# Latent attention interleaved one slice per product step, over four output and two gate chunks

## The reference, cut to what matters

```python
q, k = ...                    # 8 heads of 64 + 32 columns (the 32 rotated)
z = einsum("bhqd,bshd->bhqs", q_blk, k) * 96 ** -0.5
p = softmax(where(key_chunk <= q_chunk, z, -inf))
o_mla = einsum("bhqs,bshd->bhqd", p, v)
y_sb  = (o_sb  * silu(gate_sb))  @ w_o_sb
y_mla = (o_mla * silu(gate_mla)) @ w_o_mla
g = sigmoid(gate_logits + b_gate).reshape(b, s, 2, D_MODEL)
merged = g[:, :, 0] * y_sb + g[:, :, 1] * y_mla
x = x + merged @ w_out
```

## Time and profile before

| What | Value |
|---|---|
| median of three runs | 1740.01 us |
| the three runs | 1741.44, 1740.01, 1737.16 us |
| span of the profiled execution, first to last instruction | 1738.7 us |
| median less that span | 1.3 us |
| TensorE busy, share of the span | 96% |
| VectorE, ScalarE, GpSimd busy | 62%, 41%, 5% |
| mean granted TensorE clock | 0.981 |

### The profile page before, as it was taken

The page is one execution under the profiler, slowest core; times in us unless marked ns, Lnnn a source line. Parts: engine busy times, 40 slices in busy tenths (PEclk is TensorE's granted clock), DMA queues, the critical chain, the costliest instruction groups (busy, mean ns, idle before and its releaser), DMA issues.

```text
span 1738.7 us, 25519 instructions
## 1 busy us (share of the span) xinstructions
PE 1660.7 (96%) x9824; PEld 1332.2 (77%) x9824; DVE 1077.4 (62%) x1680; ACT 718.1 (41%) x1084; POOL 90.7 (5%) x130
## 2 busy tenths in 40 slices
PE   5979999999999999999989999999999999999997
PEld 2868787888888868777668888888887778876786
DVE  8899877665566765565655554455685563666443
ACT  4423434332333334444443332233546773655331
POOL 0063210000000000000000000000000000000000
PEclk9989999999999999999989999999999999999998
DMA  8342662434433444342222222322322211211231
GB/s 352 99 113 75 231 218 97 145 133 155 171 145 127 162 136 171 121 137 95 70 79 89 96 86 92 109 98 77 103 97 73 73 61 56 85 55 38 86 120 49
DMA packets 48821, 198.79 MB, mean 114 GB/s; under 512 B 8112, under 2 KB 13072, under 8 KB 35424
## 3 DMA queue, kind: packets, MB, share of 16 engines
q1 hardware_dynamic: 36064, 154.52, 25.8%
q0 software_dynamic: 12672, 43.10, 7.5%
HBM read 192.71 MB, written 4.23 MB: 113 GB/s over the span
## 4 chain that ended last, share of the span: by engine, by line
PE 82%; DVE 5%; ACT 5%; issue 5%; DMA 2%; POOL 1%; SPq 1%; DVEq 0%; ACTq 0%; POOLq 0%
PE ps L524 25%; PE ps L526 24%; PE ps L525 24%; ACT w_hi L983 2%; PE ps L630 2%; PE ps L643 2%; PE ps L655 2%; DMA ada<-in_ada_k 1%; PE ps L798 1%; ACT pw L1094 1%; POOL Mtz L341 1%; DVE w_lo L1454 1%; PE ps L591 1%; PE ps L774 0%; ACT sq L1085 0%
## 5 line engine op out<-in xcount | busy, mean ns | idle before, releaser
L524 PE MATMUL ps<-xn_hi,w_lo 128*128 128x512 f32 x1248 | 502.1, 402 | 11.0 <-DVE xn_lo L1604 9.2
L526 PE MATMUL ps<-xn_hi,w_hi 128*128 128x512 f32 x1248 | 491.1, 394 | 0.0
L525 PE MATMUL ps<-xn_lo,w_hi 128*128 128x512 f32 x1248 | 490.9, 393 | 0.0
L1454 DVE TENSOR_TENSOR w_lo<-raw,w_hi 128x2048 fp32r<-128x2048 f32 (+4 forms) x146 | 309.5, 2122 | 194.3 <-ACT w_hi L983 194.1
L983 ACT ACTIVATE w_hi<-raw 128x2048 fp32r<-128x2048 f32 (+4 forms) x147 | 260.9, 1775 | 175.2 <-PE ps L526 165.6
L524 PEld LDWEIGHTS ps<-xn_hi,w_lo 128*128 128x128 f32 x1248 | 237.5, 190 | 67.9 <-issue 18.5
L526 PEld LDWEIGHTS ps<-xn_hi,w_hi 128*128 128x128 f32 x1248 | 237.2, 190 | 50.8
L525 PEld LDWEIGHTS ps<-xn_lo,w_hi 128*128 128x128 f32 x1248 | 237.8, 191 | 46.2
L526 PE MATMUL ps<-act_hi,w_hi 128*128 128x512 f32 x352 | 136.9, 389 | 0.0
L524 PE MATMUL ps<-act_hi,w_lo 128*128 128x512 f32 x352 | 136.9, 389 | 0.0
L525 PE MATMUL ps<-act_lo,w_hi 128*128 128x512 f32 x352 | 136.9, 389 | 0.0
(11 more groups left out here) (396 smaller groups left out, 2430.9 us busy)
## 6 DMA issues: line engine op xcount, KB each, us to landing
raw<-in_weights SPq DMA_DIRECT2D x95, 1024.0 KB, 4.9
adaw<-in_ada_w POOLq DMA_DIRECT2D x64, 512.0 KB, 4.6
raw<-in_weights SPq DMA_DIRECT2D x18, 768.0 KB, 4.1
raw<-in_weights SPq DMA_DIRECT2D x16, 640.0 KB, 3.8
ada<-in_ada_k SPq DMA_DIRECT2D x8, 1024.0 KB, 17.9
rot<-in_ada_w POOLq DMA_DIRECT2D x16, 512.0 KB, 5.3
fbias<-f_dram SPq DMA_DIRECT2D x16, 256.0 KB, 4.0
raw<-in_weights SPq DMA_DIRECT2D x8, 512.0 KB, 3.6
```

Source lines behind the costliest of these rows:

```text
L524: pe.matmul(bank, lo_w, hi_x, start=start, stop=False)
L525: pe.matmul(bank, hi_w, lo_x, start=False, stop=False)
L526: return pe.matmul(bank, hi_w, hi_x, start=False, stop=stop)
L1454: V.tensor_tensor(w_lo[:, slot, w], raw[:, slot, w], f32(w_hi[:, slot, w]), ALU.subtract).then_inc(split_lo, 1)
```

## The change

On TensorE every product step is now followed by exactly one slice, over `osb_0` to `osb_3`, `g1_0` and `g1_1`: step, A, step, B, step, C. After the first slice that is issued ahead, 53 slices go with the first 53 of 64 steps. `g1_1` moves ahead of `omla_0`; `omla_1` follows `omla_0`; then `g1_2`, `omla_2`, `g1_3`, `omla_3` as before.

The splits move: `osb_1`, `osb_2`, `osb_3` to periods 1, 3, 6; `g1_0` to period 8 on ACT and in halves to periods 8 and 9 on DVE; `g1_1` to period 12, whole, on both; `omla_0` behind period 16 on ACT and behind period 17 on DVE. `branch_out` of the output chunks follows periods 4, 6, 9 and 12. The sigmoid of odd gate chunks goes to `nt` instead of `hn`. Behind the attention, ACT and DVE split `omla_1` ahead of the merging of 0, and `g1_2` behind it.

```diff
-for _m in range(4):
+LAYERS += [("g1_0", 8, 256, 1), ("g1_1", 8, 256, 1), ("omla_0", 4, 256, 1), ("omla_1", 4, 256, 1)]
+for _m in (2, 3):
     LAYERS += [(f"g1_{_m}", 8, 256, 1), (f"omla_{_m}", 4, 256, 1)]
...
+SPLIT_AT = (1, 3, 6, 8, 12)
...
+    def second_gate(m):
+        return (hn, nt)[m % 2]
...
         next(beats)
-        steps = [0]
         def between():
-            for _ in range(1 + steps[0] % 2):
-                next(beats, None)
-            steps[0] += 1
+            next(beats, None)
...
-        for m in range(4):
-            layer(f"g1_{m}", xn_hi, xn_lo, between=None if m else between)
-            if m == 0:
-                for _ in beats:
-                    pass
-            layer_part(f"omla_{m}", 0, mla_out(0), mla_out(1), (gm_lo, GATED["gate_mla"]) if m == 0 else None)
+        for m in range(2):
+            layer(f"g1_{m}", xn_hi, xn_lo, between=between)
+        for m in range(2):
+            layer(f"omla_{m}", mla_out(0), mla_out(1), (gm_lo, GATED["gate_mla"]) if m == 0 else None)
+        for m in range(2, 4):
+            layer(f"g1_{m}", xn_hi, xn_lo)
+            layer(f"omla_{m}", mla_out(0), mla_out(1))
...
         for n in range(18):
-            following = FIRST["osb_0"] + n // 4
-            mla_period(n, later=(lambda: split_next(following)) if n in (2, 6, 10, 14, 17) else None)
-        out_of("g1_0", gate_out(1, 0, lambda r: hn[:, r]))
-        for m in range(4):
-            if m:
-                layer(f"g1_{m}", gate_out(1, m, lambda r: hn[:, r]))
-            layer(f"omla_{m}", lambda j, b, i: None)
+            following = FIRST["osb_0"] + SPLIT_AT.index(n) if n in SPLIT_AT else None
+            mla_period(n, later=None if following is None else lambda: split_next(following))
+            if n == 16:
+                out_of("g1_0", gate_out(1, 0, lambda r: second_gate(0)[:, r]))
+                split_next(FIRST["g1_1"])
+        out_of("g1_1", gate_out(1, 1, lambda r: second_gate(1)[:, r]))
+        def merged_hi(m):
             for r in range(2):
                 act.wait_ge(m_sum, 2 * m + r + 1)
                 A(mg_hi[:, 2 * m + r], sq[:, r], ACT.Copy).then_inc(m_hi, 1)
+        for m in range(2):
+            split_next(FIRST[f"omla_{m}"])
+            merged_hi(m)
+        for m in range(2, 4):
+            layer(f"g1_{m}", gate_out(1, m, lambda r: second_gate(m)[:, r]))
+            split_next(FIRST[f"omla_{m}"])
+            merged_hi(m)
...
+        g1 = FIRST["g1_0"]
         for n in range(18):
-            following = FIRST["osb_0"] + n // 4
-            last = FIRST["g1_0"]
-            if n == 14:
-                mla_period(n, later=lambda: split_part(last // 2, last % 2, 0))
-            elif n == 15:
-                mla_period(n, later=lambda: split_part(last // 2, last % 2, 1).then_inc(split_lo, 1))
+            if n == 8:
+                mla_period(n, later=lambda: split_part(g1 // 2, g1 % 2, 0))
+            elif n == 9:
+                mla_period(n, later=lambda: split_part(g1 // 2, g1 % 2, 1).then_inc(split_lo, 1))
             else:
-                mla_period(n, later=(lambda: split_next(following)) if n in (2, 6, 10, 17) else None)
-            if n and n % 4 == 0:
-                m = n // 4 - 1
+                following = FIRST["osb_0"] + SPLIT_AT.index(n) if n in SPLIT_AT else None
+                mla_period(n, later=None if following is None else lambda: split_next(following))
+            if n in (4, 6, 9, 12):
+                m = (4, 6, 9, 12).index(n)
                 branch_out("osb", m, lambda r: mgs_of[2 * m + r])
...
+        split_next(FIRST["g1_1"])
+        def merged(m):
...
         for m in range(4):
-            if m:
+            if m >= 2:
                 layer(f"g1_{m}")
-            layer(f"omla_{m}")
+            split_next(FIRST[f"omla_{m}"])
             after_layer(dve, f"g1_{m}")
-            branch_out("omla", m, lambda r: hn[:, r])
+            branch_out("omla", m, lambda r: second_gate(m)[:, r])
...
+            merged(m)
```

More of the change, by code:

```diff
@@ L2143, in _ @@
         dve.wait_ge(sg_ready, 8)
+        g1 = FIRST["g1_0"]
         for n in range(18):
-            following = FIRST["osb_0"] + n // 4
-            last = FIRST["g1_0"]
-            if n == 14:
-                mla_period(n, later=lambda: split_part(last // 2, last % 2, 0))
-            elif n == 15:
-                mla_period(n, later=lambda: split_part(last // 2, last % 2, 1).then_inc(split_lo, 1))
-            else:
-                mla_period(n, later=(lambda: split_next(following)) if n in (2, 6, 10, 17) else None)
-            if n and n % 4 == 0:
-                m = n // 4 - 1
+            if n == 8:
+                mla_period(n, later=lambda: split_part(g1 // 2, g1 % 2, 0))
+            elif n == 9:
+                mla_period(n, later=lambda: split_part(g1 // 2, g1 % 2, 1).then_inc(split_lo, 1))
+            else:
+                following = FIRST["osb_0"] + SPLIT_AT.index(n) if n in SPLIT_AT else None
+                mla_period(n, later=None if following is None else lambda: split_next(following))
+            if n in (4, 6, 9, 12):
+                m = (4, 6, 9, 12).index(n)
                 branch_out("osb", m, lambda r: mgs_of[2 * m + r])
-        for m in range(4):
-            if m:
-                layer(f"g1_{m}")
-            layer(f"omla_{m}")
-            after_layer(dve, f"g1_{m}")
-            branch_out("omla", m, lambda r: hn[:, r])
-            j, b = last_of(f"omla_{m}")
-            dve.wait_ge(evac[b], done_value(j, 1))
+        split_next(FIRST["g1_1"])
+        def merged(m):
             for r in range(2):
-                TT(sq[:, r], mgs_of[2 * m + r], hn[:, r], ALU.add).then_inc(m_sum, 1)
+                TT(sq[:, r], mgs_of[2 * m + r], second_gate(m)[:, r], ALU.add).then_inc(m_sum, 1)
             for r in range(2):
@@ L2168, in _ @@
                 TT(mg_lo[:, 2 * m + r], sq[:, r], f32(mg_hi[:, 2 * m + r]), ALU.subtract).then_inc(m_lo, 1)
+        for m in range(4):
+            if m >= 2:
+                layer(f"g1_{m}")
+            split_next(FIRST[f"omla_{m}"])
+            after_layer(dve, f"g1_{m}")
+            branch_out("omla", m, lambda r: second_gate(m)[:, r])
+            j, b = last_of(f"omla_{m}")
+            dve.wait_ge(evac[b], done_value(j, 1))
+            merged(m)
         layer("mix_out", residual(None, "out"))
```

## The result

The changed kernel takes 1742.06 us, the kernel before 1739.03 us (medians of 20 runs each); the ratio is 1.0014, 95% interval 1.0008 to 1.0020, so it is slower by about 2.4 us (1.4 to 3.5). The medians are 3.03 us apart, the means of the 20 runs 2.40. Either is less than the 5.2 us that the prediction says a measurement can tell, so by its own division the outcome is "same", to which it gave 0.52; with 20 runs each the interval is narrow enough to show the sign. The profiled execution has a span of 1739.0 us, against 1738.7 before.

A forecast was written before the change was run, and what follows sets the result against it. TensorE, busy 96% of the span, was taken as the bound. Terms +1.4 - 0.7 - 2.5 + 4.7 + 1.6 gave +4.5 us, so 1744.5 us; range 1734.5 to 1749 us.

The forecast's parts named there:

- same: Outcome that the total time changes by less than the 5.2 us a measurement can tell; chance 0.52.
- the seams: 14 score slices on TensorE now follow a step instead of transposes, 0.10 us each: +1.4 us, bounds 0 and +2.7.
- rival 1: Filler covers the waits before slice C, if ACT's and DVE's lists set the chain's start: -5.2 us, 1734.8 us; chance 0.12.
- rival 3: TensorE's clock falls at the 2.6 us wait before slice C of period 13, losing 3.0 us: 1747.5 us; chance 0.13.
- The core: Waits before slice C stay: the chain starts with scores in slice A, and the extra step sits between C and A.
- Start: Scores of period 1 waited 0.81 us for period 0's exponentials; one step fits in: -0.7 us, bounds 0 and -0.8.
- end and small waits: Periods 14 and 15 lose a split, the last weightings and five small waits get cover: -2.5 us, bounds -1 and -3.
- Splits moved: Splits and gating on DVE delay the maxima of periods 7, 9, 10, 13: +4.7 us, bounds 0 and +6.
- Behind the attention: Third gate chunk's split now stands behind merging 0, so TensorE waits before g1_2: +1.6 us, bounds 0 and +2.2.
- What the waits before slice C cost before: In the kernel before, nine waits from 1541 to 1617 us: 4.5 us shown, 5.9 us with the modelled ends.
- rival 2: DVE starts each split earlier, so the moved splits' 4.7 us go: -0.2 us, no change, 1739.8 us; chance 0.14.

The follow-up runs named there:

- run 6: Changed kernel with gating ahead of the split, g1_1's low part split in halves, g1_2's split ahead of merging 0: stretch 104.56 us, ratio 0.9989 to the kernel before.
- runs 4 and 7: Changed kernel with steps only between A and C: stretch 105.38 us, ratio 0.9991; run 6 with that, except in the drain: 99.31 us, ratio 0.9954.
- Run 1: Changed kernel with the five splits beside the attention (osb_1 to g1_1) cut to 64 words each: stretch 106.73 us against 109.77.
- run 2: Changed kernel with the output chunks' gating issued on DVE ahead of the split in periods 6, 8 and 12: stretch 107.27 us against 109.77.
- Run 3: Changed kernel with the split of g1_2 on both engines ahead of merging 0's adding and rounding: stretch 108.13 us against 109.77.
- run 5: Kernel before with only g1_1 moved ahead of omla_0 and the new order behind the attention: stretch 109.01 us against 107.35.

## Why the prediction was right, and where its sizes were off

It was right in direction and in each mechanism but one, the seams; the measured +2.4 us is 2.1 below the forecast +4.5. That it lies within the range says little, since the range was wide enough to take in rival 1 and rival 3. The test of the forecast is its terms, and the two that were off were both too high, so nothing came right by errors that cancel.

- *The core, that the waits before slice C stay, because the new step is ahead of the chain.* Shown: 0.48 us in periods 3, 11 and 15 after, against 0.49 before, and 0.33 in periods 2 and 14; run 6, in which no late maximum reaches slice C, keeps nine such waits; runs 4 and 7, with the step inside, lose them.
- *Seams, +1.4: mis-sized.* This is the term furthest off in proportion. In the trace after, the last matmul of a step is followed by the scores 0.24 us later:

```profile
1551.00 0.48 PE L530 MATMUL ps<-osb_hi,w_lo 128*128 128x512 f32 x1
1551.31 0.39 PE L531 MATMUL ps<-osb_lo,w_hi 128*128 128x512 f32 x1
1551.54 0.39 PE L532 MATMUL ps<-osb_hi,w_hi 128*128 128x512 f32 x1
1551.78 1.88 PE L636 MATMUL ps<-m_k,m_q 96*128 96x512 f32 x4
```

  The first matmul of the step behind transposes takes 0.31 instead of 0.23 us, but starts 0.03 instead of 0.11 behind the last transpose, which makes up for it. All added switches together cost 0.4 us (97.8 less 97.4 in the table), about 0.03 for each of the 14 slices where I had 0.10. The 0.33 us of the earlier trace rows come from the other attention, where the scores' tiles have 64 rows: of its 15 scores behind such a step, 10 start 0.32 to 0.33 us behind it, too regular for a wait on another engine, and the load of their first weights starts with them. I took the nearest row and read what goes with that attention as a cost of the switch. The lower bound, nothing, was the better value. The sentence of the Trainium skill (TensorE: Matmul & The Clock Gate, Part 3) on weight loads that, read by itself, would have put this term at its upper bound, with whole weight loads exposed, is further off still; this trace disagrees with it.
- *Start, -0.7, and end and small waits, -2.5: right.* By the table, run 6 against the kernel before: 0.7 less before the scores of period 1, 1.6 less before the weightings and 0.9 less before slice C, 3.15 in all where 3.2 was forecast.
- *Splits moved, +4.7: too large by 1.2, a quarter of it.* From the starts in the trace after: period 7 +0.23 (forecast 0.5), period 9 nothing (0.3), period 10 +1.05 (1.3), period 13 2.26 (2.6), in all 3.5. The places are those forecast, each 0.25 to 0.35 too large, for two reasons. I added durations where spacings count: in the lines of DVE above a gating lasts 0.68 but the next instruction starts 0.60 behind it, and 2.21 behind a split of 2.29. That is all of the excess in period 10 and about half of it in 7 and 13. And the periods with 256-wide scores have more slack than the 0.35 and 0.4 us that I gave them: in period 9 the maximum was 0.55 us late and slice C did not wait at all, and in period 13 it was 2.8 us late and slice C 2.26. Run 1 removes 3.04 of this term, run 2 alone 2.50.
- *Behind the attention, +1.6: right.* Run 3 takes away 1.64, run 5 adds 1.66.
- *What the waits before slice C cost before*, 5.9 us, was read too low: the view of the earlier trace rows leaves out the four of 0.09 us, and from start to start all of them cost 7.1. No term of the sum uses it, but rival 1 does, which would have come out at -6.4 instead of -5.2.

Sum by the measured terms: +0.4 seams, -3.15 start, end and small waits, +3.5 splits, +1.65 behind the attention, which is the 2.4 measured. The rivals: the filler does not cover the waits where it was put (rival 1), the splits do not fall into cover (rival 2), and the clock did not fall (rival 3), though TensorE lost 2.26 us before slice C of period 13, 2.10 shown idle, where it was 2.0 and 1.84 at 190 us. That is over the two microseconds from which I had it decide, and still nothing fell. The window of that wait (busy times of TensorE, loads, DVE, ACT, POOL, then granted clock) is at the 2.4 GHz level throughout:

```profile
1603.00:1617.00 14.00, 11.49 (x67) 7.84 (x66) 9.09 (x21) 6.67 (x16) 0.00 (x0) 1.00 0.14 39
```

What stays open: why in the earlier attention the weights of the scores are loaded only when the scores start; and the order of ACT's list. The copy of slice B stands behind the exponentials of the same period although it doesn't use them. A copy ahead of them, or a second PSUM bank for slice C, might shorten the chain itself, and would put the core of this account to a harder test than moving the steps did. Neither was tried.

## What to carry to other kernels

Filler work hides a chain of waits only between the chain's first and last link on the busy engine: find the instruction that starts the chain and the one that waits for its end, and put the steps there, not evenly. Where an engine works a list strictly in order, put what is ready ahead of what waits for another engine; here that alone was worth 2.5 us of the stretch. And measure such a change by a stretch between two fixed instructions of the trace, since 2 us of 1740 drown in what happens elsewhere.

## What the runs showed of the hardware that was not expected

The start of the latent attention moved by 2.1 us between two profiles whose code up to there is the same. From the last scores of the attention before it to its own first scores, at 1541.78 and 1539.68, it is 113.57 us in the kernel before and 110.43 in the changed one. Those last scores, from the timelines of TensorE before and after:

```profile
1428.21 1.13 PE L630 MATMUL ps<-b_k,b_q 64*128 64x512 f32 x4
```

```profile
1429.25 1.13 PE L636 MATMUL ps<-b_k,b_q 64*128 64x512 f32 x4
```

The windows from 1455 to 1475 us, where sums of one column stand between dense products (TensorE, loads, DVE, ACT, POOL, then granted clock), before and after:

```profile
1455.00:1475.00 20.00, 20.00 (x89) 16.72 (x87) 3.69 (x4) 4.94 (x9) 0.00 (x0) 0.83 0.23 73
```

```profile
1455.00:1475.00 20.00, 20.00 (x106) 17.08 (x105) 5.23 (x6) 6.49 (x11) 0.00 (x0) 1.00 0.21 73
```

In the profile after the clock stays at 2.4 GHz behind the sums, in the one before it falls to 1.2 GHz for some microseconds, with the same instructions in the same order ahead of it. Of the nine profiles here two kept it (the changed kernel and run 2, 110.4 us between those scores), in the other seven it fell (113.6 to 113.7 us). So that one drop costs 3.1 to 3.3 us; ahead of it the changed kernel was 1.04 us behind, which leaves the 2.1. It is part of why single runs of one kernel differ: the 20 of the kernel before lie between 1736.48 and 1742.44 us.
